# Convolution transforms of a two-block model as three rounded products instead of f32, with a hand-placed order of steps

## What is computed

```python
def long_conv(z, filt, skip):
    seq = z.shape[1]
    zf = jnp.fft.rfft(z, n=2 * seq, axis=1)
    y = jnp.fft.irfft(zf * filt[None], n=2 * seq, axis=1)[:, :seq]
    return y + z * skip.astype(jnp.float32)

def hyena_mixer(u, conv_w, filt, skip):
    u = short_conv(u, conv_w).astype(jnp.float32)
    v, x1, x2 = jnp.split(u, 3, axis=-1)
    z = x1 * long_conv(v, filt[0], skip[0])
    return x2 * long_conv(z, filt[1], skip[1])
```

## Time and profile before

| | |
|---|---|
| median of 3 runs | 2307.05 us (2306.89 to 2307.23) |
| the profiled execution's own time | 2307.05 us |
| its span in the trace | 2305.2 us |
| PE busy | 2298.8 us (100%) |
| DVE busy | 1422.7 us (62%) |
| ACT busy | 1117.9 us (48%) |
| POOL busy | 494.5 us (21%) |
| DMA | 458.20 MB at a mean of 199 GB/s |

### The profile page before, as it was taken

How to read it: one execution, slowest core, us unless ns; L and a number is a source line. 1 busy time by engine, 2 the same in 40 slices (tenths; PEclk the granted TensorE clock), 3 DMA queues, 4 the chain that set the end, 5 groups by cost and what they waited for, 6 DMA issues and landing times.

```text
span 2305.2 us, 26456 instructions
## 1 busy us (share of the span) xinstructions
PE 2298.8 (100%) x10390; PEld 1895.2 (82%) x10390; DVE 1422.7 (62%) x1939; ACT 1117.9 (48%) x1452; POOL 494.5 (21%) x571
## 2 busy tenths in 40 slices
PE   9999999999999999999999999999999999999999
PEld 7777888888888888888888888888888888888887
DVE  6687756644556555554455555679994765466564
ACT  6444555544335444443344444544456654444653
POOL 1001011300202100100000011159997322022100
PEclk9999999999999999999999999999999999999999
DMA  9566466765546666665566566655655676655454
GB/s 337 190 195 203 149 225 208 235 221 186 171 149 215 212 225 198 197 218 196 194 199 209 193 218 212 209 183 183 198 183 184 202 240 216 188 189 154 157 173 137
DMA packets 252444, 458.20 MB, mean 199 GB/s; under 512 B 19690, under 2 KB 39877, under 8 KB 251616
## 3 DMA queue, kind: packets, MB, share of 16 engines
q1 hardware_dynamic: 238608, 432.13, 56.6%
q0 software_dynamic: 13712, 24.39, 3.8%
HBM read 431.82 MB, written 2.10 MB: 188 GB/s over the span
## 4 chain that ended last, share of the span: by engine, by line
PE 97%; DVE 1%; ACT 1%; DMA 0%; issue 0%; SPq 0%; ACTq 0%; DVEq 0%
PE ps L97 96%; PE ps L100 1%; DVE WLO L109 1%; DMA RAW<-in_w_in 0%; ACT WHI L103 0%; DVE MIX L109 0%; ACT L103 0%; DVE UU L109 0%; DVE HS L109 0%; SPq L138 0%; ACT BB L103 0%; DVE LG L109 0%; DVE QS L109 0%; ACT KS L103 0%; ACT DZ L103 0%
## 5 line engine op out<-in xcount | busy, mean ns | idle before, releaser
L109 DVE TENSOR_TENSOR WLO<-RAW,WHI 128x1024 fp32r<-128x1024 f32 x700 | 850.9, 1222 | 701.8 <-ACT WHI L103 698.6
L103 ACT ACTIVATE WHI<-RAW 128x1024 fp32r<-128x1024 f32 x793 | 835.9, 1058 | 871.2 <-PE ps L97 865.2
L97 PE MATMUL ps<-WHI,Ahi 128*128 128x512 f32 x1904 | 750.9, 395 | 0.5 <-DVE WLO L109 0.5
L97 PE MATMUL ps<-WHI,Alo 128*128 128x512 f32 x1904 | 741.7, 390 | 0.0
L97 PE MATMUL ps<-WLO,Ahi 128*128 128x512 f32 x1904 | 741.3, 390 | 0.0
L97 PEld LDWEIGHTS ps<-WHI,Ahi 128*128 128x128 f32 x1904 | 358.6, 188 | 76.8 <-issue 2.3
L97 PEld LDWEIGHTS ps<-WLO,Ahi 128*128 128x128 f32 x1904 | 358.7, 188 | 75.6 <-issue 2.3
L97 PEld LDWEIGHTS ps<-WHI,Alo 128*128 128x128 f32 x1904 | 358.5, 188 | 74.9
L109 POOL TENSOR_TENSOR WLO<-RAW,WHI 128x1024 fp32r<-128x1024 f32 x92 | 218.9, 2409 | 49.8 <-ACT WHI L103 49.4
L120 DVE SCALAR_TENSOR_TENSOR ps<-YT,GC,ps 128x256 f32<-128x256 f32 x480 | 188.8, 479 | 8.0 <-ACT ps L103 8.0
L138 POOL DMA_DIRECT2D AC<-TF x88 | 46.4, 534 | 561.8 <-DVE TF L117 558.9
(11 more groups left out here) (329 smaller groups left out, 2207.3 us busy)
## 6 DMA issues: line engine op xcount, KB each, us to landing
RAW<-in_w_gate_up SPq DMA_DIRECT2D x88, 1024.0 KB, 5.2
RAW<-in_a_w_in SPq DMA_DIRECT2D x48, 1024.0 KB, 5.1
RAW<-in_w_down SPq DMA_DIRECT2D x44, 1024.0 KB, 5.0
RAW<-in_w_in SPq DMA_DIRECT2D x39, 1024.0 KB, 5.2
RAW<-in_w_xkv SPq DMA_DIRECT2D x32, 1024.0 KB, 5.6
RAW<-in_w_kv SPq DMA_DIRECT2D x32, 1024.0 KB, 5.7
RAW<-in_b_w_in SPq DMA_DIRECT2D x32, 1024.0 KB, 5.5
RAW<-in_w_out SPq DMA_DIRECT2D x16, 1024.0 KB, 5.0
```

The source lines that it names most:

```text
L97: return self.e.matmul(o, l, r, start=start, stop=stop, skip_group_check=True)
L103: return self.e.activation(o, i, func, scale=scale, **kw)
L109: return self.e.tensor_tensor(o, a, b, op)
```

## The change

The four f32 matmuls of each `fold` and each `back` become twelve matmuls of rounded operands (hi x hi, hi x lo, lo x hi). New steps make the operands: ACT rounds (`FH_HI`, `IDF_HI`, `V_HI`, `ZA_HI`, `ZB_HI`), POOL subtracts (`FH_LO`, `IDF_LO`, `V_LO`, `ZA_LO`, `ZB_LO`, each in the place of its source; `V_LO` is a part of `MIX_LO`). V is `mixslice(2)`, the input of `fold`. Steps are moved: `fold(0)`, `zsum(0)`, both `zmul` of 0 one half later, `ymix(0)` from hy2 7 to hy2 6, `fold(1)` and `zsum(1)` two halves later, `ymix(1)` one half earlier, parts of `short(2)`; both `back` stay.

```diff
+    put("hy1", 4, ("split_fh",))
+    put("hy1", 6, ("split_idf",))
+    for n, j, i in (("hy1", 3, 0), ("hy2", 4, 1), ("qk", 3, 3)):
-    for n, j, i in (("hy1", 3, 0), ("hy2", 4, 1), ("scc", 4, 2), ("qk", 3, 3)):
         put_each(n, j, [("short", i, s) for s in range(3)])
-    put_each("hy1", 6, [("fold", 0), ("zsum", 0)])
-    put("hy2", 0, ("zmul", 0, 0))
-    put("hy2", 2, ("zmul", 0, 1))
-    put("hy2", 7, ("ymix", 0))
+    put("hy1", 5, ("split_v", 0))
+    put_each("hy1", 7, [("fold", 0)])
+    put("hy2", 0, ("zsum", 0))
+    put("hy2", 1, ("zmul", 0, 0))
+    put("hy2", 3, ("zmul", 0, 1))
+    put("hy2", 6, ("ymix", 0), ("split_z", 0))
     put("scc", 1, ("back", 0, 0), ("back", 0, 1))
-    put_each("scc", 2, [("fold", 1), ("zsum", 1)])
-    put("scc", 7, ("zmul", 1, 0))
+    put("scc", 2, ("split_v", 1))
+    put("scc", 3, ("short", 2, 0))
+    put_each("scc", 4, [("fold", 1), ("zsum", 1)])
+    put_each("scc", 6, [("short", 2, 1), ("short", 2, 2)])
+    put("sch", 0, ("zmul", 1, 0))
     put("sch", 1, ("zmul", 1, 1))
-    put("sch", 3, ("ymix", 1))
+    put("sch", 2, ("ymix", 1), ("split_z", 1))
     put("sch", 5, ("back", 1, 0), ("back", 1, 1))
...
         def fold(o):
+            e.wait_ge(*of("transform_lo", "fh"))
+            e.wait_ge(*of("transform_lo", "v", o))
...
-                    i = e.matmul(b[:, :], FH[:, t, part, :], mixslice(2)[:, t, :], True, True)
+                    e.matmul(b[:, :], FH_HI[:, t, part, :], V_HI[:, t, :], True, False)
+                    e.matmul(b[:, :], FH_HI[:, t, part, :], V_LO[:, t, :], False, False)
+                    i = e.matmul(b[:, :], FH_LO[:, t, part, :], V_HI[:, t, :], False, True)
...
         def back(o, t):
-            e.matmul(b[:, :], IDF[:, t, 0, :], re, True, False)
-            e.matmul(b[:, :], IDF[:, t, 1, :], im, False, True).then_inc(*done("pb", ("back", o, t)))
+            e.wait_ge(*of("transform_lo", "idf"))
+            e.wait_ge(*of("transform_lo", "z", o))
+            A, B = (ZA_HI, ZA_LO), (ZB_HI, ZB_LO)
+            for n, (hi, lo) in enumerate((A, B) if t == 0 else (B, A)):
+                e.matmul(b[:, :], IDF_HI[:, t, n, :], hi[:, n, :], n == 0, False)
+                e.matmul(b[:, :], IDF_HI[:, t, n, :], lo[:, n, :], False, False)
+                i = e.matmul(b[:, :], IDF_LO[:, t, n, :], hi[:, n, :], False, n == 1)
+            i.then_inc(*done("pb", ("back", o, t)))
...
+            elif what == "split_v":
+                e.wait_ge(*(of("back", 0, 1) if k else of("short", 0, 2)))
+                e.activation(V_HI[:, :, :], mixslice(2)).then_inc(*done("transform_hi", "v", k))
+            elif what == "split_z":
+                e.wait_ge(*of("ymix", k))
+                e.activation(ZA_HI[:, :, :], ZA[:, :, :])
+                e.activation(ZB_HI[:, :, :], ZB[:, :, :]).then_inc(*done("transform_hi", "z", k))
...
+            elif what == "split_v":
+                e.wait_ge(*of("transform_hi", "v", k))
+                e.tensor_tensor(V_LO, mixslice(2), f(V_HI[:, :, :]), AL.subtract).then_inc(*done("transform_lo", "v", k))
+            elif what == "split_z":
+                e.wait_ge(*of("transform_hi", "z", k))
+                e.tensor_tensor(ZA_LO[:, :, :], ZA[:, :, :], f(ZA_HI[:, :, :]), AL.subtract)
+                e.tensor_tensor(ZB_LO[:, :, :], ZB[:, :, :], f(ZB_HI[:, :, :]), AL.subtract).then_inc(*done("transform_lo", "z", k))
```

More of the change, by code:

```diff
@@ L206, in build_program @@
     ZA, ZB = at("ZA", AR + 32, [2, 512]), at("ZB", AR + 66, [2, 512])
+    FH_HI, FH_LO = at("FH_HI", AR + 38, [2, 2, 128], F32R), at("FH_LO", AR + 36, [2, 2, 128], F32R)
+    IDF_HI, IDF_LO = at("IDF_HI", AR + 46, [2, 2, 128], F32R), at("IDF_LO", AR + 44, [2, 2, 128], F32R)
+    ZA_LO, ZB_LO = at("ZA_LO", AR + 32, [2, 512], F32R), at("ZB_LO", AR + 66, [2, 512], F32R)
+    ZA_HI, ZB_HI = at("ZA_HI", AR + 76, [2, 512], F32R), at("ZB_HI", AR + 80, [2, 512], F32R)
+    V_HI, MIX_LO = at("V_HI", AR + 76, [2, 512], F32R), at("MIX_LO", AR, [2, D], F32R)
+    V_LO = MIX_LO[:, :, 1024:1536]
     CWB = at("CWB", AR + 70, [3, 512])
@@ L743, in back @@
             e.wait_ge(*free)
-            e.wait_ge(*of("ymix", o))
-            e.wait_ge(*of("d_t", 1))
-            re, im = (ZA[:, 0, :], ZB[:, 1, :]) if t == 0 else (ZB[:, 0, :], ZA[:, 1, :])
-            e.matmul(b[:, :], IDF[:, t, 0, :], re, True, False)
-            e.matmul(b[:, :], IDF[:, t, 1, :], im, False, True).then_inc(*done("pb", ("back", o, t)))
+            e.wait_ge(*of("transform_lo", "idf"))
[6 more added lines that the diff above has]
+            i.then_inc(*done("pb", ("back", o, t)))
         def gates(d):
@@ L1340, in step @@
                     e.activation(ODD[:, part, :], ring.ap(("spectrum", k, part, 1))[:, :]).then_inc(*done("odd", k, part))
+            elif what == "split_fh":
+                e.wait_ge(*of("d_fd", 2))
+                e.wait_ge(*of("odd", 1, 1))
+                e.activation(FH_HI[:, :, :, :], FH[:, :, :, :]).then_inc(*done("transform_hi", "fh"))
+            elif what == "split_idf":
+                e.wait_ge(*of("d_t", 1))
+                e.activation(IDF_HI[:, :, :, :], IDF[:, :, :, :]).then_inc(*done("transform_hi", "idf"))
+            elif what == "split_v":
[5 more added lines that the diff above has]
+                e.activation(ZB_HI[:, :, :], ZB[:, :, :]).then_inc(*done("transform_hi", "z", k))
             elif what == "fold":
@@ L1698, in short @@
                 e.wait_ge(*of("d_cw", i))
-                e.tensor_tensor(dst, U, wb(1), AL.mult).then_inc(*done("centre_tap", i))
+                e.tensor_tensor(dst, U, wb(1), AL.mult).then_inc(*done("short", i, "centre"))
                 e.wait_ge(*of("d_u", i, 1))
-                e.wait_ge(*of("centre_tap", i))
+                e.wait_ge(*of("short", i, "centre"))
                 e.tensor_tensor(UU[:, 0:2, :], UU[:, 0:2, :], wb(0), AL.mult).then_inc(*done("short", i, 0))
@@ L2183, in step @@
                 e.dma_start(TMP[0:1, 0:512], I["hy_skip"][0, 1:2, :]).then_inc(*landed("d_sk", 1))
+            elif what == "split_fh":
+                e.wait_ge(*of("transform_hi", "fh"))
+                e.wait_ge(*of("pb", ("spectrum", 1, 1)))
+                e.tensor_tensor(FH_LO[:, :, :, :], FH[:, :, :, :], f(FH_HI[:, :, :, :]), AL.subtract).then_inc(*done("transform_lo", "fh"))
+            elif what == "split_idf":
+                e.wait_ge(*of("transform_hi", "idf"))
+                e.tensor_tensor(IDF_LO[:, :, :, :], IDF[:, :, :, :], f(IDF_HI[:, :, :, :]), AL.subtract).then_inc(*done("transform_lo", "idf"))
+            elif what == "split_v":
[5 more added lines that the diff above has]
+                e.tensor_tensor(ZB_LO[:, :, :], ZB[:, :, :], f(ZB_HI[:, :, :]), AL.subtract).then_inc(*done("transform_lo", "z", k))
             elif what == "tables":
```

## The result

The changed kernel takes 2328.82 us as the median of five runs (2327.76 to 2329.61), against 2307.05 before: 21.8 us more, a ratio of 1.0094, with a 95% interval of 1.0083 to 1.0105. The prediction was 2326.8, in a range of 2317.5 to 2332.0. The profiled execution took 2327.76 us, the lowest of the five, with a span of 2325.7: 20.5 above the span before.

The account below looks back on a forecast made before the run. PE, busy for the whole span, was taken as the bound. Path delays of 13.3, POOL beside DVE 2.2 and clock 4.2 made 19.7, added to 2307.05: 2326.8 us, range 2317.5 to 2332.0.

Parts of the forecast that it names:

- PE's own work, -3.0: Two folds and two backs on PE: 13.9 us of f32 matmuls become 10.9 for 48 rounded ones.
- the rival of slow table products: Products of the tables in `fold` and `back` run no faster than f32, adding 30 us: 2357; chance 0.02.
- Step 1: `short(0)` ends at 110.86 as before, ACT rounds V, POOL subtracts until 114.3; PE waits 0.8 us at `fold(0)`.
- the 1.5 that the prediction allowed: Sign expected in the changed kernel's trace: PE waits below 1.5 us at `fold(0)`.
- The Trainium skill's rule: Two-input DVE and GpSimd instructions exclude each other throughout, whoever comes first; `FH_LO` would hold DVE, adding 1.3 us.
- Steps 2 and 3: After `fold(0)`: the `WLO` ahead of `zsum(0)` begins at 120.0, DVE takes 25.6 us, `ymix(0)` ends at 145.6.
- Step 4: `split_z` after `ymix(0)`: two roundings, two subtractions, until 152.4; PE waits 7.4 us and is through `back(0)` at 155.1.
- The wait of 7.4 + 1.1: At `back(0)`: PE waits 7.4 us for `split_z`, plus one `WLO` that holds up POOL.
- The path to `back(1)`: After `back(0)`: no wait at `fold(1)`, `ymix(1)` ends at 192.4, PE waits 7.8 us; +12.8, with hand-overs +13.3.
- The clock, +4.2: PE's clock falls to its lower level after each of two long waits, one 2.1 us loss each.
- the rival in which the clock stays up: PE's clock stays up through the waits: 2322.6 us, or 2324.7 if it falls once; chance 0.25.
- The second rival, 2330.3: POOL and DVE hold each other up everywhere and the clock falls a third time: 23.2 us more; chance 0.13.

Follow-up runs that it names:

- e11: Changed kernel with V and Z subtracted on DVE, Z in two parts, and transform steps placed otherwise; 2304.11 us, -2.9 against the kernel before.
- e6: Changed kernel with one more POOL subtraction of 128x1024 behind `zsum(0)`; 2331.65 us, +24.7 against the kernel before.
- e4: Changed kernel with sixteen dummy f32 matmuls ahead of each `back`, keeping PE busy in the waits; 2325.17 us, +18.4 against the kernel before.
- e2: Changed kernel with `back` put back to f32 and Z not split, keeping the new order and rounded `fold`; 2310.45 us, +3.7 against the kernel before.
- e7: Changed kernel with a POOL memset of 128x1024 added behind `zsum(0)`; 2329.65 us, +22.7 against the kernel before.
- e9: Changed kernel, splits still on ACT and POOL, steps placed otherwise, `back(0)` three halves later; 2318.65 us, +11.7 against the kernel before.
- e12: As e9, with `split_z(0)` moved from hy2 7 to scc 0, so POOL issues loads ahead of the subtractions; 2314.93 us, +8.0 against the kernel before.
- e8: Changed kernel with V and Z subtracted on DVE, Z in two parts, order of steps as changed; 2313.71 us, +6.8 against the kernel before.
- e5: Changed kernel with the two subtractions of `split_z` on DVE instead of POOL; 2322.11 us, +15.2 against the kernel before.

## Why the prediction was right

The forecast of 2326.8 was 2.0 too low. Its steps held in kind, and their sizes nearly so, but for `fold(0)`.

- **PE's own work, -3.0.** Right; e11 measures 2.9 with no wait around it. The new matmuls stand 0.227 to 0.233 apart, so the rival of slow table products falls.
- **Step 1, `fold(0)`: a wait of 0.8.** It was 2.28. This is the step that was mis-sized, and beyond the 1.5 that the prediction allowed. `short(0)` ended at 111.93 instead of 110.86, because POOL's `FH_LO` held a `WLO` of DVE for 1.1; most of the rest is hand-overs, 115.46 to 115.72 alone from POOL's last row to PE. I had taken POOL alone as the one that waits, from the earlier trace rows, and left the other direction out of the sum. e6 shows that DVE waits too. The Trainium skill's rule (SBUF — State Buffer, section "SBUF: two separate sides") had it, at 1.3 in the prediction; in this trace it is 1.1.
- **Steps 2 and 3.** The `WLO` ahead of `zsum(0)` was to begin at 120.0 and began at 121.54: the same 1.1 and hand-overs. From it to the end of `ymix(0)` 25.6, measured 147.17 - 121.54 = 25.6, to the tenth.
- **Step 4, `split_z(0)`.** 6.8 and one `WLO` of 1.1 in the working, 155.07 - 147.17 = 7.9 in the trace, of which 1.0 is `ZB_LO` taking 3.33 instead of 2.35. The wait of 7.4 + 1.1 was 8.35.
- **The path to `back(1)`.** No wait at `fold(1)`, as said. The stretch to the end of `ymix(1)` was 22.2 + 2.2 = 24.4 in the working and 196.95 - 172.56 = 24.4 in the trace, with DVE standing still for the emptying of scc as described. The wait of 7.8 + 1.1, part of it near sch 5, was 1.63 + 7.20.
- **The clock, +4.2.** 1.8 and 2.5 in the profiled run. e4 takes it away and gains 3.4 by the medians. The choice of one loss after each long wait held, and the rival in which the clock stays up falls. The choice rested on one row, the start of the program, between bounds of 0 and 6.3, so that some luck is in it.
- **The second rival, 2330.3.** It is right in its first half: POOL and DVE hold each other up, both ways. Its third fall of the clock was to come behind the late `WLO` of sch 5; none is there, but e2, e6 and e7 show one behind `fold(0)`. The measured median lies between the forecast and this rival.

In the profiled run the forecast was short by 0.8 (span 2324.9 against 2325.7): 20.9 instead of 19.7 at `back(1)`, less the 0.4 that the prediction, with everything behind `back(1)` moving along, did not have. Against the median another 1.1 is missing. A fall of the clock behind `fold(0)`, as in e2, would be of that size, and the lower granted clock of the higher runs fits; that it stood there in those runs is not shown.

The expected gain of 3.0 was there all the time. It was covered by waits in a place where PE had one microsecond to spare and the change put 7.9 of serial work.

## What to carry to other kernels

When an f32 product is cut into rounded products, price the making of the operands as a chain (rounding, then subtraction, then the first matmul) from the last input to the first use, and compare it with the room that the full engine has there; the saving in matmuls is all that can be won, and each microsecond of chain beyond the room is lost, with 1.6 to 2.7 us more here for each wait behind which the clock fell. Put such a chain on the fastest engine for it, in parts as the inputs come, and move the use later only after looking at what stands in each queue behind the moved step: in e9 the move removed a wait of 8.2 us at `back(0)` and brought one of 6.4 at `fold(1)`, in part through two loads behind two subtractions.

## What was not expected of the hardware

- The granted clock fell behind quite short waits, and not each time: behind 1.78, 2.43 and 2.60 us in e12, 2.11 in e2, e6 and e7, 2.78 in e8; it stayed up behind 1.78 and 2.50 in e9 and behind 2.11 in the changed kernel, e4 and e5. After the short waits it could fall when PE was already at work again: 1.5 us after the restart in e2, 1.1 in e8. A loss was 1.6 us (e8, e12) to 2.7 us (e9, behind the 6.39, the record after `fold(1)` included).
- A POOL subtraction holds DVE for less than its own row: 1.70 for one of 128x1024 (e6) that takes 2.35 where nothing holds it up, and 1.1 for `FH_LO`, 128x512, whose row of 2.19 began beside the DVE instruction before. The rule in the prediction has the whole instruction; these rows show less.
